# Linear attention in a two-block fp32 model: one level product for both token halves, the diagonal as row sums, the stage reordered

## The reference, cut to what matters

```python
def step(S, inp):
    qi, ki, vi, gi = inp
    b = jnp.cumsum(gi, axis=-2)
    b_last = b[:, :, -1:, :]
    o_inter = jnp.einsum('bhtc,bhcv->bhtv', qi * jnp.exp(b), S)
    diff = b[:, :, :, None, :] - b[:, :, None, :, :]
    decay = jnp.exp(jnp.where(causal, diff, -jnp.inf))
    attn = jnp.einsum('bhtsc,bhsc->bhts', qi[:, :, :, None, :] * decay, ki)
    o_intra = jnp.einsum('bhts,bhsv->bhtv', attn, vi)
    S = jnp.exp(b_last[:, :, 0, :])[..., None] * S + jnp.einsum('bhsc,bhsv->bhcv', ki * jnp.exp(b_last - b), vi)
    return S, o_inter + o_intra
```

## Time and profile before

| | us |
|---|---|
| median of 3 runs | 2322.52 |
| lowest, highest | 2321.79, 2324.61 |
| the profiled execution | 2323.65 |
| its span, first to last instruction | 2321.8 |
| PE busy (matmul) in it | 2305.2 |
| DVE busy | 1522.8 |
| ACT busy | 1244.6 |

### The profile page before, as it was taken

How to read it: one execution, slowest core, us unless ns; L and a number is a source line. 1 busy time by engine, 2 the same in 40 slices (tenths; PEclk the granted TensorE clock), 3 DMA queues, 4 the chain that set the end, 5 groups by cost and what they waited for, 6 DMA issues and landing times.

```text
span 2321.8 us, 29386 instructions
## 1 busy us (share of the span) xinstructions
PE 2305.2 (99%) x11924; PEld 1956.6 (84%) x11924; DVE 1522.8 (66%) x2085; ACT 1244.6 (54%) x1506; POOL 0.2 (0%) x4
## 2 busy tenths in 40 slices
PE   8999999999999999999999999999999999999999
PEld 7887888888888788888888888788888887878887
DVE  6764566765774556775775675777667657566773
ACT  6544445555654444654654665465455547555652
POOL 0000000000000000000000000000000000000000
PEclk9999999999999999999999999999999999999999
DMA  7556455655555455565556543445655555244553
GB/s 252 192 195 219 154 178 177 198 197 184 182 201 189 150 177 191 179 201 199 175 188 216 181 150 118 163 162 184 208 168 191 204 174 177 97 146 163 191 190 127
DMA packets 175803, 417.25 MB, mean 180 GB/s; under 512 B 16658, under 2 KB 21266, under 8 KB 175668
## 3 DMA queue, kind: packets, MB, share of 16 engines
q1 hardware_dynamic: 175380, 415.24, 53.4%
q10 hardware_dynamic: 288, 0.14, 0.0%
HBM read 414.27 MB, written 1.05 MB: 179 GB/s over the span
## 4 chain that ended last, share of the span: by engine, by line
PE 95%; DVE 2%; ACT 1%; DMA 1%; issue 1%; SPq 0%; ACTq 0%; DVEq 0%
PE psum L659 27%; PE psum L595 16%; PE psum L597 16%; PE psum L596 16%; PE psum L660 14%; PE psum L627 2%; PE psum L933 1%; PE psum L759 1%; DVE split_w L1612 0%; ACT split_w L1153 0%; DMA raw<-t_gate_up_1a_dram 0%; DMA x<-x_dram 0%; PE psum L909 0%; PE psum L776 0%; PE psum L919 0%
## 5 line engine op out<-in xcount | busy, mean ns | idle before, releaser
L1612 DVE TENSOR_TENSOR split_w<-raw,split_w 128x2048 fp32r<-128x2048 f32 (+2 forms) x408 | 887.1, 2179 | 348.5 <-ACT split_w L1153 346.9
L659 PE MATMUL psum<-xt,split_w 128*128 128x512 f32 x2816 | 984.4, 394 | 2.6 <-DVE split_w L1612 1.6
L1153 ACT ACTIVATE split_w<-raw 128x2048 fp32r<-128x2048 f32 (+2 forms) x408 | 741.0, 1824 | 304.7 <-PE psum L597 292.4
L660 PE MATMUL psum<-xt,split_w 128*128 128x256 f32 x2816 | 787.9, 280 | 0.0
L659 PEld LDWEIGHTS psum<-xt,split_w 128*128 128x128 f32 x2816 | 527.5, 187 | 124.5 <-DVE split_w L1612 1.8
L660 PEld LDWEIGHTS psum<-xt,split_w 128*128 128x128 f32 x2816 | 531.9, 189 | 0.3
L595 PE MATMUL psum<-split_w,xt 128*128 128x512 f32 (+1 forms) x736 | 291.3, 396 | 0.0
L597 PE MATMUL psum<-split_w,xt 128*128 128x512 f32 (+1 forms) x736 | 283.8, 386 | 0.0
L596 PE MATMUL psum<-split_w,xt 128*128 128x512 f32 (+1 forms) x736 | 283.6, 385 | 0.0
L595 PE MATMUL psum<-split_w,ht_hi 128*128 128x512 f32 x700 | 272.9, 390 | 0.0
L597 PE MATMUL psum<-split_w,ht_lo 128*128 128x512 f32 x700 | 272.5, 389 | 0.0
(11 more groups left out here) (262 smaller groups left out, 1783.9 us busy)
## 6 DMA issues: line engine op xcount, KB each, us to landing
raw<-w_in_dram SPq DMA_DIRECT2D x180, 512.0 KB, 4.5
raw<-t_gate_up_1b_dram SPq DMA_DIRECT2D x88, 512.0 KB, 4.6
raw<-t_gate_up_2a_dram SPq DMA_DIRECT2D x88, 512.0 KB, 4.6
raw<-t_gate_up_2b_dram SPq DMA_DIRECT2D x88, 512.0 KB, 4.5
raw<-t_gate_up_1a_dram SPq DMA_DIRECT2D x85, 512.0 KB, 4.7
raw<-ffn_w_down_dram SPq DMA_DIRECT2D x80, 512.0 KB, 4.4
raw<-w_a_dram SPq DMA_DIRECT2D x40, 512.0 KB, 4.2
raw<-w_b_dram SPq DMA_DIRECT2D x40, 512.0 KB, 4.5
```

The costliest lines, as they stand in the source:

```text
L659: nc.tensor.matmul(bank, whi[:, slot, w], xt[:, c, :, :], start=c == 0, stop=False)
L660: last = nc.tensor.matmul(bank[:, 0:T], wlo[:, slot, w], xt_hi[:, c, :], start=False, stop=c == DC - 1)
L1153: nc.scalar.activation(whi[:, u % HL, first:n], raw[:, r, first:n], ACT.Copy).then_inc(hi_done, 1)
L1612: nc.vector.tensor_tensor(wlo[:, u % HL, first:n], raw[:, r, first:n], whi[:, u % HL, first:n], ALU.subtract).then_inc(w_ready, 1)
```

## The change

The keys of one token half and the queries of the other now lie in one tile. `sm[:, lv, 0]` holds, in the places of the even blocks, the keys of half 0, and in those of the odd blocks the queries of half 1; `sm[:, lv, 1]` holds the rest, the queries of half 0 and the keys of half 1. One product of the two gives the weights of half 0 in the places above the diagonal and those of half 1, turned, below it. So `weights(h, i)` has four levels each and i runs over 0 and 1. The masks `pairs` take both. VectorE collects the products in `pgx` [128, 128]; from it the upper part is copied to `pg[:, 0]`, and PE turns `pgx` whole (`turned(h)`, a transposition), from which VectorE copies the upper part to `pg[:, 1]`. Level 7, the product between halves, is the fourth of `weights(h, 1)`, and VectorE copies it to `px`. The diagonal is set by scaling the identity by `own`, the row sums of q times k, made once a layer; for that q as tokens goes to a tile of its own, `qtok`. The exponentials go to `expo`, one buffer for all heads, and VectorE multiplies them into `sm`.

The stage is reordered on the three engines, the list of banks with it. The norm of the heads is made in two parts: heads 0 to 2 (`out_norm(0)`, `out_scaled(0, 3)`) and head 3. The transfers are not changed.

The tables:

```diff
+SO_PARTS = (slice(0, 6), slice(6, 8))
...
-FOUR_BANKS = SMALL_OPS.index(("weights", 1, 2))
+FOUR_BANKS = SMALL_OPS.index(("ob", 1))
...
-        pairs.append((s // (2 * n) == q // (2 * n)) & (s // n % 2 == 0) & odd)
+        pairs.append((s // (2 * n) == q // (2 * n)) & (s // n != q // n))
...
-    out["t_pairs"] = np.concatenate(pairs + [s == q], axis=1)
+    out["t_pairs"] = np.concatenate(pairs + [s < q], axis=1)
```

PE:

```diff
                 def weights(h, i):
 
-                    eng.wait_ge(done, e.after(done, ("decayed", h, i // 2)))
+                    eng.wait_ge(done, e.after(done, ("decayed", h, i)))
                     out = bank(("weights", h, i))
-                    for k in range(2):
-                        for m in range(MT):
...
+                    for k in range(4):
+                        lv = 4 * i + k
+                        last = nc.tensor.matmul(out[:, k * P:(k + 1) * P], sm[:, lv, 0, :], sm[:, lv, 1, :],
+                                                start=True, stop=True)
                     last.then_inc(small, e.mark(small, ("weights", h, i)))
 
-                def cross(h):
...
+                def turned(h):
+
+                    eng.wait_ge(done, e.after(done, ("weights", h, 1)))
+                    nc.tensor.transpose(bank(("turned", h))[:, 0:P], pgx[:, :], ident[:, :]).then_inc(
+                        small, e.mark(small, ("turned", h)))
 
                 def linear_out(h):
-                    eng.wait_ge(done, e.after(done, ("weights", h, 3)))
-                    eng.wait_ge(acted, e.after(acted, ("cross", h)))
+                    eng.wait_ge(done, e.after(done, ("turned", h)))
```

PE, the wait ahead of the first product with w_proj_b:

```diff
                 eng.wait_ge(done, e.after(done, ("merged", "a", 1)))
-                eng.wait_ge(done, e.after(done, ("obt", 1)))
+                eng.wait_ge(done, e.after(done, ("obt", 0)))
                 wide(u, 0, OB, 0, 1)
```

VectorE:

```diff
+                    if i == 0:
+                        for m in range(MT):
+                            ins = nc.vector.tensor_scalar(pg[:, m, :], ident[:, :], own[:, 4 * m + h:4 * m + h + 1], None,
+                                                          ALU.mult)
...
+                    if i == 1:
+                        nc.vector.tensor_copy(px[:, :], level[:, 3, :])
+                    for k in range(4 - i):
+                        ins = nc.vector.copy_predicated(pgx[:, :], pairs[:, 4 * i + k, :].bitcast(I32), level[:, k, :])
...
+                    if i == 1:
+                        nc.vector.copy_predicated(pg[:, 0, :], pairs[:, LEVELS - 1, :].bitcast(I32), pgx[:, :])
+
+                def turned(h):
...
-                for u in (11, 12, 13):
-                    split(u0 + u)
+                split(u0 + 11)
+                split(u0 + 12)
+                eng.wait_ge(acted, e.after(acted, ("tok2", "qb")))
+                e.link(nc.vector.tensor_tensor(qk_prod[:, :, :], qtok[:, :, :], tok2[:, :, :], ALU.mult))
+                e.link(nc.vector.tensor_reduce(own[:, :], qk_prod[:, :, :].rearrange("p m (h d) -> p (m h) d", h=GLA_HEADS),
+                                               axis=AX_X, op=ALU.add))
+                nc.vector.tensor_scalar(own[:, :], own[:, :], DK ** -0.5, None, ALU.mult).then_inc(
+                    done, e.mark(done, ("own",)))
+                split(u0 + 13)
```

More of the change, by code:

```diff
@@ L1018, in mix2_tensor @@
                 wide(u, 0, XT, 1, 2)
-                weights(0, 2)
-                weights(0, 3)
-                cross(0)
+                exponents(1, 0)
                 prob_turn(5)
                 wide(u, 0, XT, 2, 3)
-                exponents(1, 0)
+                turned(0)
+                exponents(1, 1)
                 eng.wait_ge(acted, e.after(acted, ("prob_t", 5)))
@@ L1028, in mix2_tensor @@
                 wide(u, 0, XT, 3, 4)
-                exponents(1, 1)
                 u += 2
@@ L1048, in mix2_tensor @@
                 blocks(u, 0, 2, OA, (0,), True, False, False)
-                weights(1, 2)
+                linear_out(1)
                 blocks(u, 1, 2, OA, (1,), False, False, True)
[L1051 to L1056, removed]
+                blocks(u + 1, 0, 2, OA, (2, 3), False, True, True)
+                weights(2, 0)
                 u += 2
@@ L1405, in decays @@
                 def decays(h, part):
-                    if h >= 2:
-                        eng.wait_ge(small, e.after(small, ("cross", h - 2)))
+                    if (h, part) == (0, 0):
+                        eng.wait_ge(done, e.after(done, ("own",)))
+                    if h:
+                        eng.wait_ge(done, e.after(done, ("decayed", h - 1, part)))
                     for m in range(MT):
-                        copied(("ex", h, part, m), xg[:, h % 2, 4 * part:4 * part + 4, m * P:(m + 1) * P],
+                        copied(("ex", h, part, m), expo[:, part, :, m * P:(m + 1) * P],
                                bank(("ex", h, part, m)).rearrange("p (l t) -> p l t", l=4), func=ACT.Exp)
-                def cross(h):
-                    if h:
-                        eng.wait_ge(small, e.after(small, ("ob", h - 1)))
-                    copied(("cross", h), px[:, :], bank(("cross", h))[:, 0:P])
                 def out_squares(h):
@@ L1426, in out_squares, with so_root @@
                     last.then_inc(acted, e.mark(acted, ("so", h)))
+                def so_root(i):
+                    cols = SO_PARTS[i]
+                    eng.wait_ge(done, e.after(done, ("so", i)))
+                    nc.scalar.activation(so[:, 2, cols], so[:, 1, cols], ACT.Sqrt).then_inc(
+                        acted, e.mark(acted, ("so_root", i)))
                 def hi_turned(hi, label, first, gain=None):
@@ L1992, in gated, with out_norm, out_scaled @@
                     ins.then_inc(done, e.mark(done, ("ob", h)))
+                def out_norm(i):
+                    cols = SO_PARTS[i]
+                    eng.wait_ge(done, e.after(done, ("ob", cols.stop // 2 - 1)))
+                    nc.vector.tensor_scalar(so[:, 1, cols], so[:, 0, cols], 1.0 / DV, EPS, ALU.mult, ALU.add).then_inc(
+                        done, e.mark(done, ("so", i)))
+                    eng.wait_ge(acted, e.after(acted, ("so_root", i)))
+                    e.link(nc.vector.reciprocal(so[:, 2, cols], so[:, 2, cols]))
+                    rsqrt_newton(so[:, 3, cols], so[:, 1, cols], so[:, 2, cols], so[:, 4, cols], ("rso", i))
+                def out_scaled(first, end):
+                    for h in range(first, end):
+                        for m in range(MT):
+                            part = rb[:, m, h * DV:(h + 1) * DV]
+                            ins = nc.vector.tensor_scalar(part, part, so[:, 3, 2 * h + m:2 * h + m + 1], None, ALU.mult)
+                    ins.then_inc(done, e.mark(done, ("obn", first)))
                 def merge(branch, n, p, u):
```

184 lines of the change are left out of this document (83 added, 101 removed).

## The result

The changed kernel takes 2329.86 us (median of 8 runs, 2328.74 to 2330.86), beside 2322.67 us for the kernel before on the same chip (8 runs). The ratio is 1.0031, 95% interval 1.0020 to 1.0042: slower by 7.2 us, and 2.4 us above the range of the prediction.

A forecast was written before the change was run, and what follows sets the result against it. TensorE, busy 99% of the span, was taken as the bound. Removing 15.1 us of products, mostly given back as waits, left 0.6 us saved: forecast 2321.9 us, 8 in 10 range 2317.0 to 2327.5 us.

The forecast's parts named there:

- The removed work: TensorE's level products: 18 instructions go and one transposition comes per head, saving 1.89 us a head, 15.1 us for the kernel.
- The work of the other engines: VectorE gains nothing, 3.6 us a head; row sums cost nothing; ScalarE has three more table loads a layer, 1.28 us each.
- VectorE rival: Slower multiplications and predicated copies on VectorE lengthen (b) by 3.1 us a layer, giving 2328.2 us; chance 0.08.
- The five waits: New TensorE waits in each layer between the first level product and the turning of `merged`: 1.0, 2.1, 2.1, 4.6, 1.2 us.
- (c): Second half of `exponents(3, 0)`: TensorE waits 2.1 us for bank 6, until VectorE has copied `turned(2)`.
- a: Behind `exponents(2, 1)`: TensorE waits 1.0 us for banks 4 and 5, which ScalarE must first read.
- (b): At `turned(2)`: TensorE waits 2.1 us for VectorE's level copies of head 2.
- (d): First w_proj_b product: TensorE waits 4.5 us for the low part of ("obt", 0), 4.6 with 0.1 of waiting before.
- e: Turning of `merged`: TensorE waits 1.2 us for merge ("b", 0) on VectorE.
- The sum of 107.8 to 108.1 us: First level product to turning of `merged`, per layer: 108.4 us before; 107.8 by sum, 108.1 by schedule, 0.3 us less.
- The clock: Rival: TensorE drops to 1.2 GHz in wait (d), losing about 1.9 us behind it per layer, giving 2325.7 us; chance 0.16.
- the sign that the prediction had named: TensorE's pitch of 0.45 us behind (d) would show the clock case and the forecast wrong.

The follow-up runs named there:

- best: Changed kernel with instruction lists reordered on VectorE and TensorE against all five forecast waits, no operation dropped: 2303.57 us, 0.9915 of the kernel before.
- warm_all: Changed kernel with unread identity transpositions put on TensorE inside waits (b), (c) and (d): 2321.68 us, 0.9994 of the kernel before.
- warm_c: Changed kernel with unread identity transpositions on TensorE inside wait (c) alone: 2325.78 us, 1.0012 of the kernel before.
- warm_bc: Changed kernel with unread identity transpositions on TensorE inside waits (b) and (c), (d) left idle: 2325.97 us, 1.0010 of the kernel before.
- fix_b: Changed kernel with VectorE's list reordered at waits (b) and (c) alone, taking them away: 2317.74 us, 0.9976 of the kernel before.
- no_own: Changed kernel without the row sums of queries times keys on VectorE: 2328.86 us, 1.0027 of the kernel before.
- b_wait: Kernel before, with nine unread additions on VectorE that make TensorE wait at the first w_proj_b product: 2335.37 us, 1.0053 of the kernel before.
- fix_d: Changed kernel with VectorE's list reordered at wait (d) alone: 2318.27 us, 0.9979 of the kernel before.
- warm_d: Changed kernel with unread identity transpositions on TensorE inside wait (d) alone: 2325.46 us, 1.0009 of the kernel before.
- b_wait_warm: b_wait with 36 identity transpositions on TensorE inside the added wait: 2333.08 us, 1.0041 of the kernel before.
- best2: best with split(28) ahead of the low part of the first turned chunk on VectorE: 2302.04 us, 0.9913 of the kernel before.

## Why the prediction was wrong

**The removed work.** Right. Where no new wait comes, from the first level product to the turning of the first attention output, PE took 22.84 us before and takes 21.00 now: 1.84 for one head, against 1.89. That stretch has 147 instructions before and 130 now, the 17 fewer that were forecast for a head. In best the stage is 9.86 us shorter, which is the forecast's 7.6 us of removed work and 2.3 of the 4.0 us of waits of before.

**The work of the other engines.** Right. The predicated copy of 128x128 takes 300 ns (taken at 0.31), the multiplication with reversed halves 285 ns:

```profile
L1962 DVE TENSOR_TENSOR sm<-expo,qbt 128x128 f32<-128x128 f32 x64 | 18.2, 285 | 0.0
L1979 DVE COPY_PREDICATED pgx<-pairs,psum 128x128 f32<-128x128 int32 x56 | 16.8, 300 | 7.9 <-PE psum L932 6.4
```

So the VectorE rival falls, and `own` is hidden, with 1.8 us to spare. The table loads take 1.28 us each, as in the earlier trace rows.

**The five waits.** Right to 0.3 us each, but for (c). With the 0.16 us of the modelled end they are 0.97 (a, forecast 1.0), 2.37 (b, 2.1), 1.57 and 2.10 (c, 2.1), 4.61 (d, 4.6) and 1.15 us (e, 1.2). In layer 0 (c) is shorter since the half rate already ran inside it. The sum of 107.8 to 108.1 us holds when the clock does: 107.7 in warm_all.

**The clock.** This is the step that failed: the sum has no term for products at half rate. The runs show 8.2 us of them, 41 products that start 0.427 in place of 0.227 us apart, and the fillers take just that away. The mechanism stood among the rivals ("Chance 0.16", "about 1.9 us are lost behind (d) in each layer"), and its price behind (d) was right (about 1.5 and 2.1 us; the pitch of 0.43 us there is the sign that the prediction had named). But it was given too small a chance and only one place. The statement that no wait of before in running work was over 1 us is wrong: there is one of 1.38 us, early in the program, and the clock behind it is full.

```profile
40.67 0.47 PE L659 MATMUL psum<-xt,split_w 128*128 128x512 f32 x1 [1.38 <-DVE split_w L1612]
...
41.00:44.00 3.00, 3.00 (x19) 1.00 0.73 216
```

That still said nothing of waits of 2 and 4.6 us, while the only row that bore on these, the first 16 transpositions at half rate, spoke for the rival. And (b) and (c), though only three instructions lie between them, got no price for the clock at all: from the last product ahead of (b), at 1435.44, to the first behind (c), at 1440.78, PE started those three. The products at half rate behind (c) cost another 1.8 and 2.8 us, more than those behind (d). With the clock's loss taken at both places and at its measured size, the sum gives 2321.9 + 8.2 = 2330.1.

The Trainium skill has a related case ("TensorE: Matmul & The Clock Gate", A second HAM failure mode): in a bf16 kernel that cycled through PSUM banks, frequent short idle pieces between groups of products made the clock go back and forth between its levels. The trace is in line with it at (b) and (c), where no single wait was over 2.21 us and the clock went to 0.50, though these are two waits and not many short ones. I had drawn on the page's other section and left this one out.

## What to carry to other kernels

A wait on the bounding engine costs its length and what the engine loses behind it. Where a change puts a wait of 2 us or more into running matrix work, or two with little between them, allow for up to 3 us more for products at half rate (here 1.5 to 2.8 us a place, and once nothing behind a wait of 2.2 us), and don't take the full clock of a trace without such waits as evidence against it. A saving on the bounding engine that only becomes waits has not been lost: the lists of the engines that it waits for must be reordered with it, here for 26 us, 8.2 of them the clock's. If a wait can't be removed, dummy transpositions in it are worth trying: they cost nothing while it lasts and the clock is full.

## What the runs showed of the hardware

- A single idle wait of 2.2 us lowered the granted clock in one layer and not in the other of the same program (warm_c). Waits of 4.45 and 5.30 us lowered it in all twelve places where they stood idle (after, warm_bc, warm_c, fix_b, no_own, b_wait, two layers each). Waits of 1.38 us (before) and 0.98 us (fix_d, best) did not.
- At the lower level a 512-column product comes every 0.427 us, at the upper every 0.227 us. Behind waits of equal length, 4.45 us, between 7.5 and 13 products ran at the lower one (wait (d): 7.5 in layer 0 of after, 13 in layer 0 of warm_c).
- fp32 transpositions of 128x128, one every 0.11 us, kept the granted clock at 1.00 in the waits of warm_all, warm_d and b_wait_warm. Right behind an idle wait of 2.2 us, in layer 0 of warm_c, they did not stop its fall.
- At the start of the program the granted clock prints 1.00 while 16 such transpositions come 0.23 us apart (before); the pitch is the surer sign there.
- The part ahead of the stage took 1387.3 to 1390.3 us from program to program. So medians can differ by some 2 us apart from what the stages show: best and best2 by 1.5 with equal stages, b_wait and b_wait_warm by 2.3 where the stages differ by 4.7. That limits what a median of this kernel can settle.
